# Between two decoder layers: squares on GpSimd, weight splits behind three sigmoids, and fillers of 512 and 256 columns

## The chip, the cores and the metric

The kernel runs on 1 core of a Trainium2 chip. The metric is the device time of one execution in microseconds (us). The engines of the core that matter here are TensorE (PE in the profile, with PEld for its weight loads), VectorE (DVE), ScalarE (ACT), GpSimd (POOL) and the queue of SyncE (SP) that issues the loads.

## The reference

One inference step of a decoder with two layers, 320 tokens (a prompt of 256 and 8 samples of 8), 1024 features. Each layer is four sub-layers with a norm before and after each; the last one is the one that the change touches:

```python
def rmsnorm(x, g):
    return x * lax.rsqrt(jnp.mean(x * x, axis=-1, keepdims=True) + EPS) * g
...
for i in range(DEPTH):                      # DEPTH = 2
    f = swiglu(rmsnorm(h, P['g_f1_pre'][i]), ...)
    h = h + 0.5 * rmsnorm(f, P['g_f1_post'][i])
    mo = mixer(rmsnorm(h, P['g_mix_pre'][i]), ...)
    h = h + rmsnorm(mo, P['g_mix_post'][i])
    f = swiglu(rmsnorm(h, P['g_f2_pre'][i]), ...)
    h = h + 0.5 * rmsnorm(f, P['g_f2_post'][i])
    gate = jax.nn.sigmoid(rmsnorm(h, P['g_ple_pre'][i]) @ P['w_ple_gate'][i])
    h = h + rmsnorm((p[i] @ P['w_ple_proj'][i]) * gate, P['g_ple_post'][i])
return rmsnorm(h, P['g_final'])
```

## The kernel before

Activations lie with features on the 128 partitions and the 320 tokens along the free dimension, so a row of 1024 features is 8 tiles of 128x320. Every product is made of three fp32r matmuls (high part by high part, high by low, low by high), so each weight and each activation is split into a high part (a copy on ScalarE, `w_hi_sb`, `x_hi`) and a low part (a subtraction on VectorE, `w_lo_sb`, `x_lo`). All order is written out by hand: each engine has its own program, and counting semaphores join them.

Weights stream through four slots (j = 0 to 3) of 128x1024. For each half, SyncE loads `raw`, ScalarE's `split` copies it to `w_hi_sb`, VectorE's `split` makes `w_lo_sb`, and TensorE uses it. A slot's next high part waits until TensorE is done with that slot (`halves_done`), and SyncE reloads `raw` when the low parts of its two slots are there (`w_lo`).

The phase `pg` is the product with `w_ple_gate`: two pairs of four halves, one output tile m = 0 to 7 for each half. For each tile VectorE takes the product out of PSUM (`move` into `ga`, semaphore `moved`), ScalarE applies the sigmoid (`sg`), and VectorE multiplies the tile of `gate` by it (`embed`, semaphore `ple_out`). The norm behind it (`post4`) needs the sum of squares of all 8 tiles of `gate`. Before the change ScalarE squares tiles 0 to 6 (`square`, into one of two buffers `sq`), VectorE adds them into `ssq` (`add_square`, semaphore `summed`), and VectorE squares tile 7 itself (semaphore `squared`). TensorE sums both over partitions (`sums`: three matmuls on `ssq` after `summed`, three on `sq` after `squared`), ScalarE takes the root (`finish_root`), VectorE inverts it (`invert`), TensorE spreads it over the partitions (`spread`), and VectorE's `boundary` scales and adds the 8 tiles to `h` and starts the next layer's first product (`first_pair` of the phase `f1_up`). Its first three weight halves (slots 0 to 2) have to be split before it, the fourth comes later.

`keep_warm` issues matmuls whose result nobody reads (fillers), with as many columns as it is told. They stand in TensorE's program between the steps of `sums` and `spread`, behind the waits that come before them. After the first sub-layer (`post1`, once in each layer) there are fillers before and after `spread` too.

Layer 1 is the last one: it ends in another way (`L == LAST`), and there is one such passage from `pg` to the next layer's `f1_up` in the whole program.

Of the kernel before, what the change touches and what calls it, by code (L numbers as in the profile page):

```python
# [110 lines left out]
def trunk(nc, x, par, side, early, w_proj, g_rows, streams, y, states):  # L111
    with ExitStack() as ctx:
# [119 lines left out]
        pool_sq = sem("pool_sq")  # L232
        x_lo_pool = sem("x_lo_pool")
# [226 lines left out]
        def _(pe):  # L460
            WARM_SIG, WARM_ROOT, WARM_X = 6, 3, 9
# [103 lines left out]
            def sums(L, name):  # L565

                n = WT if name == "ln" else DT
                tailed = name in TAILED
                pe.wait_ge(summed, v_sq(L, name, n - 1))
                for t in range(3):  # L570
                    mm = pe.matmul(ps[:, STATB, t:t + 1], ssq[:, t * P:(t + 1) * P], ones[:, 0:1], start=t == 0,  # L571
                                   stop=not tailed, skip_group_check=True)
                if tailed:

                    if name == "post4":
                        keep_warm(WARM_ROOT)
                    pe.wait_ge(squared, v_sq(L, name, n - 1))
                    for t in range(3):
                        n = min(P, T - t * P)
                        mm = pe.matmul(ps[0:n, STATB, t:t + 1], sq[:, 1, t * P:t * P + n], ones[:, 0:1], start=False,  # L580
                                       stop=True, skip_group_check=True)
                mm.then_inc(stat_full, 1)
# [132 lines left out]
            for L in range(DEPTH):  # L715
# [10 lines left out]
                keep_warm(WARM_ROOT)  # L726
                spread(L, "post1")
                keep_warm(WARM_X, T // 2)
# [85 lines left out]
                if L < LAST:  # L814
                    keep_warm(WARM_SIG)
                    sums(L, "post4")
                    keep_warm(WARM_ROOT)
                    spread(L, "post4")
                    keep_warm(WARM_X, T // 2)
# [5 lines left out]
        def _(act):  # L825
# [203 lines left out]
            for L in range(DEPTH):  # L1029
# [94 lines left out]
                for m in range(DT):  # L1124
                    if m == 2:
                        split(L, "pg", 1, 3)
                    sigmoid(sg[:, m % RING3, :], ga[:, m % 2, :], L, "pg", m)
                    for q in ((m - 1,) if m < 4 else (m - 1, m) if m == 4 else (m,) if m < DT - 1 else ()):
                        if q >= 0:
                            act.wait_ge(ple_out, L * DT + q + 1)  # L1130
                            square(gate[:, q, :], L, "post4", q, q % 2)
                            if L == LAST:
                                gain(L, q)
                    if 4 <= m < DT - 1:
                        if nxt_layer:
                            split(*nxt_layer, m - 4)
                        else:
                            keep_turned(m - 2)
# [28 lines left out]
        def _(dve):  # L1167
# [39 lines left out]
            def boundary(L, n, b, post, pre, gain, nxt):  # L1207
# [31 lines left out]
                if n == 3:  # L1239
                    split(*nxt, 1)  # L1240
# [5 lines left out]
                if n == 3:  # L1246
                    split(*nxt, 2)
# [174 lines left out]
            for L in range(DEPTH):  # L1422
# [139 lines left out]
                for m in range(DT):  # L1562
# [8 lines left out]
                    if 2 <= m <= 4:  # L1571
                        add_square(L, "post4", m - 2, m % 2)
                    if m >= 4:
                        add_square(L, "post4", m - 1, (m - 1) % 2)
# [4 lines left out]
                    if m in (1, 3):  # L1579
                        split(L, "pg", 1, 2 if m == 1 else 3)  # L1580
                    if m == 5 and nxt_layer:
                        split(*nxt_layer, 0)
                dve.wait_ge(ple_out, L * DT + DT)
                dve.wait_ge(summed, v_sq(L, "post4", DT - 3))
                if L == LAST:
                    dve.tensor_tensor(LAST_SQ[:, 0:T], gate[:, DT - 1, :], gate[:, DT - 1, :], ALU.mult)
                    dve.tensor_tensor(LAST_SQ[:, T:TPAD], gate[:, DT - 1, 2 * P:T], gate[:, DT - 1, 2 * P:T], ALU.mult).then_inc(squared, 1)
                else:
                    dve.tensor_tensor(sq[:, 1, :], gate[:, DT - 1, :], gate[:, DT - 1, :], ALU.mult).then_inc(squared, 1)
# [20 lines left out]
        def _(pool):  # L1610
# [21 lines left out]
            def boundary_x(L, n):  # L1632
                for m in POOL_X:
# [4 lines left out]
                    if n == 2 and m:  # L1638
# [4 lines left out]
                        pool.tensor_tensor(CHASE_SQ[0], CHASE_SQ[0], CHASE_SQ[i], ALU.add).then_inc(pool_sq, 1)  # L1643

# [62 lines left out]
            for L in range(DEPTH):  # L1707
# [84 lines left out]
                if L + 1 < DEPTH:  # L1792
                    boundary_x(L, 3)
# [125 lines left out]
```

## Time and profile before

| what | value |
|---|---|
| three timed executions | 1550.05, 1550.15 and 1550.22 us (median 1550.15) |
| span of the profiled execution, first to last instruction | 1547.5 us |
| median of the timed executions above that span | 2.65 us |
| TensorE busy | 1530.3 us, 99% of the span |
| VectorE, ScalarE, GpSimd busy | 1038.2, 717.9 and 652.3 us (67%, 46%, 42%) |
| mean granted TensorE clock | 0.995 of full |

The profiled execution has no total listed apart from its span; what lies around the span (start and end of the program) is taken from the timed executions. A line such as L1172 is a line of the kernel; the line of a helper stands for all its uses. In a timeline a row has the start, the duration, the engine, the line, the operation with output and inputs, and in brackets how long the engine had been idle and who released it.

### The profile page before, as it was taken

The numbers are of one execution on the slowest core, as the hardware profiler recorded it, in microseconds if no ns is written. First come the engines' busy times: TensorE is split into PE (matmuls) and PEld (weight loads), VectorE is DVE, ScalarE is ACT, GpSimd is POOL, SyncE is SP. The second block draws the span as 40 slices with busy tenths as digits, with TensorE's granted clock in tenths as the row PEclk, the third lists the DMA queues.
The fourth block names the chain that finished last, engine by engine and source line by source line (L and its number), as shares of the span: only waits on it lengthen the run. The fifth ranks groups of instructions, "written<-read, shape, count | busy, mean of one in ns | idle before, by whom it ended". The sixth has DMA issues, their size and how long they took to land.

```text
span 1547.5 us, 27988 instructions
## 1 busy us (share of the span) xinstructions
PE 1530.3 (99%) x10370; PEld 1521.0 (98%) x10370; DVE 1038.2 (67%) x1577; ACT 717.9 (46%) x1064; POOL 652.3 (42%) x693
## 2 busy tenths in 40 slices
PE   9999999999999999999999999999999999999997
PEld 9999999999999999999999999999999999999997
DVE  7555437999886755634885554389998876555356
ACT  6333335445466433433663333355455654334346
POOL 3755203499321555500147551045973317554011
PEclk9999999999999999999999999999999999999998
DMA  6444432444443544532334454334444335445422
GB/s 221 163 160 173 180 129 82 164 144 157 163 148 110 186 162 137 209 141 102 125 129 161 145 193 169 119 109 141 160 163 137 132 125 191 157 140 204 143 73 82
DMA packets 53208, 229.29 MB, mean 148 GB/s; under 512 B 3856, under 2 KB 3984, under 8 KB 49040
## 3 DMA queue, kind: packets, MB, share of 16 engines
q1 hardware_dynamic: 52560, 226.07, 42.6%
q10 hardware_dynamic: 576, 2.26, 0.4%
q8 instruction: 45, 0.74, 0.2%
q14 instruction: 27, 0.22, 0.0%
HBM read 225.27 MB, written 3.04 MB: 148 GB/s over the span
## 4 chain that ended last, share of the span: by engine, by line
PE 95%; DVE 3%; issue 1%; ACT 1%; POOL 0%; DVEq 0%; POOLq 0%; ACTq 0%
PE ps L467 29%; PE ps L469 29%; PE ps L468 29%; PE ps L509 1%; PE ps L505 1%; PE ps L506 1%; DVE h L1222 1%; DVE ga L1217 0%; DVE w_lo_sb L1172 0%; PE ps L541 0%; POOL x_lo L1637 0%; PE ps L646 0%; PE ps L587 0%; PE ps L571 0%; PE ps L647 0%
## 5 line engine op out<-in xcount | busy, mean ns | idle before, releaser
L1172 DVE TENSOR_TENSOR w_lo_sb<-raw,w_hi_sb 128x1024 fp32r<-128x1024 f32 (+1 forms) x388 | 552.9, 1426 | 227.5 <-ACT w_hi_sb L832 227.0
L467 PE MATMUL ps<-x_hi,w_hi_sb 128*128 128x320 f32 x2232 | 693.3, 311 | 1.7 <-DVE w_lo_sb L1172 1.7
L832 ACT ACTIVATE w_hi_sb<-raw 128x1024 fp32r<-128x1024 f32 (+1 forms) x388 | 429.1, 1111 | 564.6 <-PE ps L469 477.5
L469 PE MATMUL ps<-x_hi,w_lo_sb 128*128 128x320 f32 x2232 | 689.6, 309 | 0.0
L468 PE MATMUL ps<-x_lo,w_hi_sb 128*128 128x320 f32 x2232 | 689.6, 309 | 0.0
L467 PEld LDWEIGHTS ps<-x_hi,w_hi_sb 128*128 128x128 f32 x2232 | 419.0, 188 | 4.0 <-DVE w_lo_sb L1172 2.5
L468 PEld LDWEIGHTS ps<-x_lo,w_hi_sb 128*128 128x128 f32 x2232 | 419.0, 188 | 0.8
L469 PEld LDWEIGHTS ps<-x_hi,w_lo_sb 128*128 128x128 f32 x2232 | 419.0, 188 | 0.0
L467 PE MATMUL ps<-mid_hi,w_hi_sb 128*128 128x320 f32 x704 | 217.4, 309 | 0.0
L468 PE MATMUL ps<-mid_lo,w_hi_sb 128*128 128x320 f32 x704 | 217.4, 309 | 0.0
L469 PE MATMUL ps<-mid_hi,w_lo_sb 128*128 128x320 f32 x704 | 217.4, 309 | 0.0
L1637 POOL TENSOR_TENSOR x_lo<-pmf,x_hi 128x320 fp32r<-128x320 f32 x14 | 14.4, 1027 | 404.0 <-ACT pmf L879 251.5
L1622 POOL TENSOR_TENSOR gb<-ga,gb 128x320 f32<-128x320 f32 x88 | 79.9, 908 | 213.9 <-DVE gb L1299 213.8
L1625 POOL TENSOR_TENSOR gb<-gb,sg 128x320 f32<-128x320 f32 x88 | 146.2, 1661 | 15.6 <-POOL gb L1622 12.6
L1299 DVE TENSOR_TENSOR ga<-ps,rb 128x320 f32<-128x320 f32 x168 | 81.5, 486 | 95.9 <-PE ps L469 68.1
L467 PEld LDWEIGHTS ps<-mid_hi,w_hi_sb 128*128 128x128 f32 x704 | 132.2, 188 | 0.0
L469 PEld LDWEIGHTS ps<-mid_hi,w_lo_sb 128*128 128x128 f32 x704 | 132.2, 188 | 0.0
L468 PEld LDWEIGHTS ps<-mid_lo,w_hi_sb 128*128 128x128 f32 x704 | 132.2, 188 | 0.0
L1372 DVE SCALAR_TENSOR_TENSOR ps<-cbuf,cur,ps 128x256 f32<-128x256 f32 x348 | 108.1, 378 | 0.0
L1299 DVE TENSOR_TENSOR gb<-ps,rb 128x320 f32<-128x320 f32 x104 | 50.7, 487 | 55.5 <-PE ps L469 55.4
L1630 POOL TENSOR_TENSOR mid_lo<-gb,mid_hi 128x320 f32 x88 | 81.6, 927 | 14.7 <-POOL mid_hi L1628 14.7
L837 ACT ACTIVATE sq<-ps 128x320 f32<-128x320 f32 x48 | 21.0, 437 | 113.8 <-PE ps L469 113.8
(223 smaller groups left out, 1642.8 us busy)
## 6 DMA issues: line engine op xcount, KB each, us to landing
raw<-in_w_f_up SPq DMA_DIRECT2D x86, 1024.0 KB, 5.2
raw<-in_w_f_dn SPq DMA_DIRECT2D x32, 1408.0 KB, 6.0
raw<-in_w_gate SPq DMA_DIRECT2D x24, 1024.0 KB, 5.2
raw<-in_w_out SPq DMA_DIRECT2D x12, 1024.0 KB, 5.3
raw<-in_w_glu SPq DMA_DIRECT2D x8, 1024.0 KB, 5.2
raw<-in_w_short SPq DMA_DIRECT2D x8, 1024.0 KB, 5.3
raw<-in_w_wo SPq DMA_DIRECT2D x8, 1024.0 KB, 5.3
raw<-in_w_pg SPq DMA_DIRECT2D x8, 1024.0 KB, 5.3
```

Of the source, the lines that this page charges most:

```text
L467: pe.matmul(out, whi, rhs_hi, start=start, stop=False, skip_group_check=True)
L468: pe.matmul(out, whi, rhs_lo, start=False, stop=False, skip_group_check=True)
L469: return pe.matmul(out, wlo, rhs_hi, start=False, stop=stop, skip_group_check=True)
L505: pe.matmul(out, w_hi_sb[:, j, w], x_hi[:, k, :], start=k == 0, stop=False, skip_group_check=True)
L832: act.activation(w_hi_sb[:, j, 0:n], raw[:, j, 0:n], ACT.Copy).then_inc(w_hi, 1)
L837: act.activation(sq[:, par, :], src, ACT.Square).then_inc(squared, 1)
L1172: dve.tensor_tensor(w_lo_sb[:, j, 0:n], raw[:, j, 0:n], w_hi_sb[:, j, 0:n].bitcast(F32), ALU.subtract).then_inc(w_lo, 1)
L1299: dve.tensor_tensor(out, ps[:, bank, 0:T], rb[:, :], ALU.mult).then_inc(moved, 1)
L1372: dve.scalar_tensor_tensor(dst, src, cur[:, c:c + 1], before, ALU.mult, ALU.add).then_inc(tap, 1)
L1622: pool.tensor_tensor(gb[:, g, :], ga[:, g, :], gb[:, g, :], ALU.mult).then_inc(swi, 1)
L1625: pool.tensor_tensor(gb[:, g, :], gb[:, g, :], sg[:, g, :], ALU.mult).then_inc(swi, 1)
L1630: pool.tensor_tensor(lo, gb[:, g:g + 1, :], hi.bitcast(F32), ALU.subtract).then_inc(mid_ready, 1)
```

## The change

In the passage from layer 0 to layer 1, GpSimd squares tiles 0 to 6 of `gate` and adds them up (new function `gate_squares`), two instructions for each tile but the first; ScalarE no longer squares there and VectorE no longer adds. ScalarE's high parts for the next layer's slots 0, 1 and 2 stand right behind the sigmoids of tiles 3, 5 and 6, and VectorE's low parts behind the `embed` of tiles 5 (slot 0) and 6 (slots 1 and 2), where the latter two stood in `boundary` before. The fourth half of `pg` is split one tile earlier on both engines. The fillers get new numbers and widths, and those ahead of the first three matmuls of `sums` go. Layer 1 keeps its own way of doing all this, but for the fillers of `post1`.

```diff
-            WARM_SIG, WARM_ROOT, WARM_X = 6, 3, 9
+            WARM_SIG, WARM_SQRT, WARM_X, WARM_COLS = 6, 2, 5, 512
+            WARM_ROOT, WARM_ROOT_COLS = 4, 256
...
                     if name == "post4":
-                        keep_warm(WARM_ROOT)
+                        keep_warm(WARM_SIG, WARM_COLS)
                     pe.wait_ge(squared, v_sq(L, name, n - 1))
...
                 sums(L, "post1")
-                keep_warm(WARM_ROOT)
+                keep_warm(WARM_ROOT, WARM_ROOT_COLS)
                 spread(L, "post1")
-                keep_warm(WARM_X, T // 2)
+                keep_warm(WARM_X, WARM_COLS)
...
                 if L < LAST:
-                    keep_warm(WARM_SIG)
                     sums(L, "post4")
-                    keep_warm(WARM_ROOT)
+                    keep_warm(WARM_SQRT, WARM_COLS)
                     spread(L, "post4")
-                    keep_warm(WARM_X, T // 2)
+                    keep_warm(WARM_X, WARM_COLS)
...
                 for m in range(DT):
-                    if m == 2:
+                    if m == (1 if nxt_layer else 2):
                         split(L, "pg", 1, 3)
                     sigmoid(sg[:, m % RING3, :], ga[:, m % 2, :], L, "pg", m)
+                    if nxt_layer:
+                        if m in (3, 5, 6):
+                            split(*nxt_layer, {3: 0, 5: 1, 6: 2}[m])
+                        continue
...
-                if n == 3:
-                    split(*nxt, 1)
                 invert(L, post)
...
-                if n == 3:
-                    split(*nxt, 2)
                 dve.wait_ge(bc_full, v_bc(L, post))
...
-                    if m in (1, 3):
-                        split(L, "pg", 1, 2 if m == 1 else 3)
-                    if m == 5 and nxt_layer:
-                        split(*nxt_layer, 0)
+                    if m == 1:
+                        split(L, "pg", 1, 2)
+                    if m == (2 if nxt_layer else 3):
+                        split(L, "pg", 1, 3)
+                    if nxt_layer and m in (5, 6):
+                        for j in ((0,), (1, 2))[m - 5]:
+                            split(*nxt_layer, j)
...
+            def gate_squares(L):
+
+                wait_alone(stat_full, v_stat(L, "pre3"))
+                for q in range(DT - 1):
+                    if q:
+                        wait_alone(summed, v_sq(L, "post4", q - 1))
+                    pool.wait_ge(ple_out, L * DT + q + 1)
+                    pool.tensor_tensor(sq[:, 0, :] if q else ssq[:, 0:T], gate[:, q, :], gate[:, q, :], ALU.mult
+                                       ).then_inc(pool_square if q else summed, 1)
+                    if q:
+                        pool.wait_ge(pool_square, L * (DT - 2) + q)
+                        pool.tensor_tensor(ssq[:, 0:T], ssq[:, 0:T], sq[:, 0, :], ALU.add).then_inc(summed, 2 if q == DT - 2 else 1)
```

VectorE, layer 0, from the `move` of tile 5 to the first step of `boundary`; as it was before (rows on `ssq` are `add_square`; the first row on `w_lo_sb` is slot 0, the one behind `sq<-gate` slot 1, and slot 2 follows behind a reciprocal):

```order
L1299 TENSOR_TENSOR ga<-ps,rb 128x320
L1186 TENSOR_TENSOR ssq<-ssq,sq 128x320
L1559 TENSOR_TENSOR gate<-gate,sg 128x320
L1172 TENSOR_TENSOR w_lo_sb<-raw,w_hi_sb 128x1024
L1299 TENSOR_TENSOR ga<-ps,rb 128x320
L1186 TENSOR_TENSOR ssq<-ssq,sq 128x320
L1559 TENSOR_TENSOR gate<-gate,sg 128x320
L1299 TENSOR_TENSOR ga<-ps,rb 128x320
L1186 TENSOR_TENSOR ssq<-ssq,sq 128x320
L1559 TENSOR_TENSOR gate<-gate,sg 128x320
L1589 TENSOR_TENSOR sq<-gate 128x320
L1172 TENSOR_TENSOR w_lo_sb<-raw,w_hi_sb 128x1024
```

The same place with the change; the row x2 holds slots 1 and 2:

```order
L1296 TENSOR_TENSOR ga<-ps,rb 128x320
L1556 TENSOR_TENSOR gate<-gate,sg 128x320
L1173 TENSOR_TENSOR w_lo_sb<-raw,w_hi_sb 128x1024
L1296 TENSOR_TENSOR ga<-ps,rb 128x320
L1556 TENSOR_TENSOR gate<-gate,sg 128x320
L1173 TENSOR_TENSOR w_lo_sb<-raw,w_hi_sb 128x1024 x2
L1296 TENSOR_TENSOR ga<-ps,rb 128x320
L1556 TENSOR_TENSOR gate<-gate,sg 128x320
L1590 TENSOR_TENSOR sq<-gate 128x320
L1191 RECIPROCAL rinv<-root 128x3
```

The additions are gone, and the splits of slots 1 and 2 moved from behind the square of tile 7 to ahead of tile 7's `move`.

TensorE at the end of `pg` in layer 0, before (the last product of `pg`, then fillers on `pw_hi`, `sums` on `ssq` and `sq`, `spread` on `rinv`, and the first product of `f1_up`):

```order
L469 MATMUL ps<-x_hi,w_lo_sb 128x320
L563 MATMUL ps<-p_hi,pw_hi 128x320 x6
L571 MATMUL ps<-ones,ssq 128x1 x3
L563 MATMUL ps<-p_hi,pw_hi 128x320 x3
L580 MATMUL ps<-ones,sq 128x1 x2
L580 MATMUL ps<-ones,sq 64x1
L563 MATMUL ps<-p_hi,pw_hi 128x320 x3
L594 MATMUL ps<-ident,rinv 128x128 x3
L563 MATMUL ps<-p_hi,pw_hi 128x160 x9
L505 MATMUL ps<-x_hi,w_hi_sb 128x320
```

The same place with the change:

```order
L471 MATMUL ps<-x_hi,w_lo_sb 128x320
L573 MATMUL ps<-ones,ssq 128x1 x3
L565 MATMUL ps<-p_hi,pw_hi 128x512 x6
L582 MATMUL ps<-ones,sq 128x1 x2
L582 MATMUL ps<-ones,sq 64x1
L565 MATMUL ps<-p_hi,pw_hi 128x512 x2
L596 MATMUL ps<-ident,rinv 128x128 x3
L565 MATMUL ps<-p_hi,pw_hi 128x512 x5
L507 MATMUL ps<-x_hi,w_hi_sb 128x320
```

No filler stands between `pg` and the matmuls on `ssq` any more, and the six between those on `ssq` and those on `sq` are 512 columns wide.

## Rows read from the trace of the kernel before

**Rows 1.** The page: chain that ended last, share of the span by engine.

```profile
PE 95%; DVE 3%; issue 1%; ACT 1%; POOL 0%; DVEq 0%; POOLq 0%; ACTq 0%
```

**Rows 2.** Timeline of PE from the end of `pg` to `f1_up`.

```profile
764.44 1.04 PE L563 MATMUL ps<-p_hi,pw_hi 128*128 128x320 f32 x6
766.06 0.83 PE L571 MATMUL ps<-ones,ssq 128*128 128x1 f32 x6 [0.58 <-DVE ssq L1186]
...
767.83 0.91 PE L580 MATMUL ps<-ones,sq 128*128 128x1 f32 x6 [0.40 <-DVE sq L1589]
...
769.63 0.84 PE L594 MATMUL ps<-ident,rinv 128*128 128x128 f32 x3
770.12 2.19 PE L563 MATMUL ps<-p_hi,pw_hi 128*128 128x160 f32 x9
772.15 0.61 PE L505 MATMUL ps<-x_hi,w_hi_sb 128*128 128x320 f32 x1
```

**Rows 3.** Timeline of DVE in the same passage.

```profile
752.77 0.49 DVE L1559 TENSOR_TENSOR gate<-gate,sg 128x320 f32<-128x320 f32 x1 [0.42 <-ACT sg L932]
753.18 1.22 DVE L1172 TENSOR_TENSOR w_lo_sb<-raw,w_hi_sb 128x1024 fp32r<-128x1024 f32 x1
...
764.83 0.48 DVE L1299 TENSOR_TENSOR ga<-ps,rb 128x320 f32<-128x320 f32 x1
765.51 0.49 DVE L1186 TENSOR_TENSOR ssq<-ssq,sq 128x320 f32<-128x320 f32 x1 [0.20 <-issue]
766.76 0.49 DVE L1559 TENSOR_TENSOR gate<-gate,sg 128x320 f32<-128x320 f32 x1 [0.76 <-ACT sg L932]
767.28 0.49 DVE L1589 TENSOR_TENSOR sq<-gate 128x320 f32<-128x320 f32 x1
...
770.51 0.49 DVE L1217 TENSOR_TENSOR ga<-gate,ps 128x320 f32<-128x320 f32 x1 [0.15 <-PE ps L594]
```

**Rows 4.** Timeline of ACT around the sigmoid of tile 7.

```profile
765.33 1.04 ACT L832 ACTIVATE w_hi_sb<-raw 128x1024 fp32r<-128x1024 f32 x1
766.27 0.45 ACT L932 ACTIVATE sg<-ga 128x320 f32<-128x320 f32 x1
```

**Rows 5.** Windows: stretch, its us, busy of PE, PEld, DVE, ACT, POOL, then PEclk.

```profile
768.00:769.00 1.00, 1.00 (x7) 0.97 (x8) 0.91 (x1) 0.25 (x3) 0.00 (x0) 0.65 0.09 16
775.00:776.00 1.00, 1.00 (x8) 1.00 (x8) 0.96 (x3) 1.00 (x3) 0.12 (x1) 0.93 0.00 0
```

**Rows 6.** Two lines of POOL (duration min/median/max in ns), and POOL's timeline there.

```profile
L1622 POOL TENSOR_TENSOR gb<-ga,gb x88: 876/887/1865, 27.9 to 1416.3; 128x320 f32<-128x320 f32 x88
...
L1628 POOL CAST mid_hi<-gb x88: 451/452/1395, 30.9 to 1419.8; 128x320 f32 x88
...
772.45 0.87 POOL L1637 TENSOR_TENSOR x_lo<-pmf,x_hi 128x320 fp32r<-128x320 f32 x1 [28.25 <-ACT pmf L879]
```

**Rows 7.** Timeline of POOL, three instructions elsewhere in layer 0 and 1.

```profile
439.58 1.06 POOL L1783 TENSOR_TENSOR cc<-cc,sg 128x320 f32<-128x320 f32 x1 [0.26 <-DVE cc L1529]
...
736.46 0.88 POOL L1637 TENSOR_TENSOR x_lo<-pmf,x_hi 128x320 fp32r<-128x320 f32 x1 [1.63 <-ACT pmf L879]
...
853.35 1.67 POOL L1625 TENSOR_TENSOR gb<-gb,sg 128x320 f32<-128x320 f32 x1 [0.16 <-POOL gb L1622]
```

**Rows 8.** Timeline of DVE at the same three moments.

```profile
439.42 1.56 DVE L1532 TENSOR_TENSOR cc<-cc,sg 128x320 f32<-128x320 f32 x2
...
736.49 0.48 DVE L1217 TENSOR_TENSOR ga<-f,ps 128x320 f32<-128x320 f32 x1
...
852.83 1.45 DVE L1172 TENSOR_TENSOR w_lo_sb<-raw,w_hi_sb 128x1024 fp32r<-128x1024 f32 x1 [0.60 <-ACT w_hi_sb L832]
```

**Rows 9.** Timeline of PE behind the first sub-layer of layer 0.

```profile
243.44 0.54 PE L594 MATMUL ps<-ident,rinv 128*128 128x128 f32 x3
243.74 1.21 PE L563 MATMUL ps<-p_hi,pw_hi 128*128 128x160 f32 x9
245.60 0.39 PE L505 MATMUL ps<-x_hi,w_hi_sb 128*128 128x320 f32 x1 [0.65 <-DVE x_hi L1257]
```

More of the change, by code:

```diff
@@ L232, in trunk @@
         pool_sq = sem("pool_sq")
+        pool_square = sem("pool_square")
         x_lo_pool = sem("x_lo_pool")
@@ L1131, in _ @@
                             square(gate[:, q, :], L, "post4", q, q % 2)
-                            if L == LAST:
-                                gain(L, q)
+                            gain(L, q)
                     if 4 <= m < DT - 1:
[L1135 to L1138, printed above, removed]
+                        keep_turned(m - 2)
                 act.preload_act_table(ACT.Sqrt)
@@ L1570, in _ @@
                         embed(m - 1)
-                    if 2 <= m <= 4:
+                    if 2 <= m <= 4 and L == LAST:
                         add_square(L, "post4", m - 2, m % 2)
                     if m >= 4:
-                        add_square(L, "post4", m - 1, (m - 1) % 2)
+                        if L == LAST:
+                            add_square(L, "post4", m - 1, (m - 1) % 2)
                         if L == LAST and m == DT - 1:
@@ L1578, in _ @@
                         embed(m)
-                    if m in (1, 3):
-                        split(L, "pg", 1, 2 if m == 1 else 3)
-                    if m == 5 and nxt_layer:
-                        split(*nxt_layer, 0)
+                    if m == 1:
[5 more added lines that the diff above has]
+                            split(*nxt_layer, j)
                 dve.wait_ge(ple_out, L * DT + DT)
-                dve.wait_ge(summed, v_sq(L, "post4", DT - 3))
                 if L == LAST:
+                    dve.wait_ge(summed, v_sq(L, "post4", DT - 3))
                     dve.tensor_tensor(LAST_SQ[:, 0:T], gate[:, DT - 1, :], gate[:, DT - 1, :], ALU.mult)
@@ L1588, in _ @@
                 else:
-                    dve.tensor_tensor(sq[:, 1, :], gate[:, DT - 1, :], gate[:, DT - 1, :], ALU.mult).then_inc(squared, 1)
+                    dve.tensor_tensor(sq[:, 1, :], gate[:, DT - 1, :], gate[:, DT - 1, :], ALU.mult).then_inc(squared, DT)
                 if nxt_layer:
@@ L1792, in _ @@
                 if L + 1 < DEPTH:
+                    gate_squares(L)
                     boundary_x(L, 3)
```

## The prediction, made before the changed kernel ran

> **What bounds the kernel now.** I read the chain that ended last first: TensorE holds 95% of it [rows 1]. An edit on the other engines can only pay where TensorE waits for them. The change touches one such place, the passage from `pg` of layer 0 to `f1_up` of layer 1, and the fillers of `post1`; so I read TensorE's timeline there next. The fillers behind the last product start at 764.44, the first product of layer 1 at 772.15 [rows 2]: 7.7 us in which TensorE does nothing that counts. All that the change can win or lose lies there.
>
> What ends those waits: the matmuls on `ssq` start at 766.06, when VectorE's last addition ends (765.51 + 0.49 = 766.00), those on `sq` at 767.83, when tile 7's square ends (767.28 + 0.49 = 767.77) [rows 2, 3]. Behind them root, reciprocal and `spread` run to VectorE's first step at 770.51, and from there it is 772.15 - 770.51 = 1.64 us to the product [rows 2, 3]. So the chain is: tile 7's `move` (764.83), its sigmoid (766.27), its `embed` (766.76), its square. The sigmoid could have followed the `move` at 765.31, but ScalarE's weight split stood ahead of it from 765.33 on [rows 3, 4]; that costs about 0.9 us. The clock: 0.65 of full over 768 to 769 means that it fell to half (1.2 GHz) at about 768.3, and 0.93 over 775 to 776 that it rose to 2.4 GHz at about 775.1 [rows 5]; TensorE had gaps before the fall and ran almost without any before the rise. GpSimd is idle for 28 us until 772.45 [rows 6].
>
> **The change, part by part.** Removed: seven squares on ScalarE, seven additions on VectorE. Taken alone that frees the chain: the sigmoid of tile 7 no longer stands behind a split.
>
> GpSimd's new work is 13 instructions on 128x320. One such instruction takes 0.88 us where nothing disturbs it [rows 6], and the next, which waits for its result, starts 0.16 us later [rows 7]; where the semaphore goes through `wait_alone` I take 0.20. So a tile costs 0.88 + 0.16 + 0.88 + 0.20 = 2.1 us, against 0.49 on VectorE. Tile 0's `embed` ends at 753.26 [rows 3], tile 1's about 755.2, and six tiles from there end at 755.4 + 6 x 2.1 = about 767.8 even if nothing disturbs them: 1.8 us after the 766.00 of now. GpSimd sets the time of `ssq`, not the sigmoids.
>
> It will be disturbed. A GpSimd instruction at 853.35 took 1.67 us, 0.79 over its 0.88, while VectorE's split ran from 852.83 to 854.28: it got going 0.14 us before the split's end [rows 7, 8]. At 439.58 one took 1.06, and the second of two VectorE products, asked for at about 439.83, ended at 439.42 + 1.56 = 440.98, where two alone take 0.9: here VectorE waited for GpSimd [rows 7, 8]. At 736.46 one took its plain 0.88 beside a VectorE instruction that read PSUM (736.49) [rows 7, 8]. So instructions of the two engines that read two SBUF tiles take turns, in order of asking. In this passage VectorE has such ones in plenty: eight `embed`, tile 7's square (0.49 each) and five splits (1.22 each) [rows 3].
>
> I walked through the passage with these durations: turns in order of asking, handed over 0.14 us before the end, other waits as in the rows. The splits of `pg` hold up tiles 0 and 1 (tile 0's square ends 755.1, tile 1's addition 758.4). Additions 2 to 6 then end at about 760.6, 763.8, 767.0, 769.9 and 772.0. VectorE is held up in its turn: slot 0's split ends at 763.1, `embed` 6 at 764.5, the splits of slots 1 and 2 at 766.3 and 768.1, and only then come tile 7's `move` (768.5 against 765.31 now), its sigmoid (769.0), `embed` (770.2) and square (771.3). With 0.16 in place of 0.20 the two ends are 771.3 and 772.2; with handovers from 0.05 to 0.3 us before the end, 770.5 to 774 and 769.4 to 773. I take **772.0 for `ssq`**, square of tile 7 at or ahead of it.
>
> The Trainium skill's page "SBUF — State Buffer", section "Who interferes with whom", says that the second engine blocks fully until the first finishes. The rows at 853.35 show 0.14 us less than that [rows 7, 8]. By the page's rule the same walk ends at 774.0 and the time below would be 2 us longer.
>
> Next TensorE. Its program now has no filler between `pg` (764.44) and the wait for `ssq`, so it stands idle for 7.5 us, longer than any gap now, and the clock is at half when the matmuls on `ssq` start. Six fillers of 512 columns follow. They were to cover the wait for tile 7's square, but that square is there already: they stand on the path. No row has 512 columns: six of 320 took 1.04 us, of which about 0.15 each and 0.3 for the last to drain [rows 2], so 512 columns are 0.24 us at full clock by the ratio of columns and 0.47 at half; I bound one by 0.15 (as 320) and 0.47. From 772.0 at half clock: six passes on `ssq` 1.4 (0.83 at full clock, scaled by `spread`, 0.84 against 0.54 [rows 2, 9], and up to double), fillers 2.8, passes on `sq` 1.4, root and reciprocal as now (768.74 to 769.25, 0.5) while two more fillers run 0.9, `spread` 0.84, then 1.64 to the product: 781.0, which is 8.8 later than 772.15. All at full clock: 0.83 + 1.4 + 0.83 + 0.5 + 0.54 + 1.64 = 5.7, so 777.8, 5.6 later. In the passage as it is now the clock came back to full while such matmuls ran without gaps [rows 5], so I expect it back somewhere within these 9 us and take 7.0, the middle. The next layer's first tiles then run at full clock, but GpSimd's `x_lo` tiles at 772.45 and after still pace them [rows 6]: 0.2 back.
>
> Nothing else counts. Behind GpSimd's squares the next layer's `x_lo` tiles are queued; the first of them waits for the first `h` tile, which comes 5 us after the squares are done. In `post1` TensorE's nine fillers end at 244.95 and it waits for `x_hi` until 245.60 [rows 9]; five of 512 take 1.3 us from 243.74 and end at 245.04, still before. Four of 256 columns have 1024 in all, where three of 320 have 960: 0.03 us. If that cover were gone, each `post1` would cost 0.1. Loads: slot 2 was split at 765.33 without a wait for its load [rows 4]; its load now starts about 1.1 us earlier, with the earlier split of `pg`'s fourth half, and the split comes no more than that earlier. ScalarE's extra splits lie between sigmoids where it is idle; the one between sigmoids 0 and 1 delays `embed` 1 by nothing, since VectorE is in a split until 754.40 [rows 3].
>
> Sum: + 7.0 - 0.2 = + 6.8 us. The span of the profiled execution, 1547.5, becomes 1554.3; the timed median lies 2.65 above the span, so 1550.15 + 6.8 = **1557.0 us**. From TensorE's start in layer 1 all is bound by TensorE as before, so that the shift stays to the end.
>
> **The rivals.**
>
> *GpSimd and VectorE don't hinder each other here.* Then `ssq` is there at 767.8 and tile 7's square at 767.2. Speaks for it: many GpSimd instructions keep the 0.88, the median of L1622 is 887 ns [rows 6]. Against: the stretched ones fall just where VectorE reads two SBUF tiles [rows 7, 8]. The time: 767.8 + 5.7 = 773.5 at full clock (+ 1.3), or, since the clock now falls at 768.3 anyway, the fillers at half, up to + 3.6. So 1551.5 to 1553.8, 1552.3 as the likeliest.
>
> *GpSimd keeps pace, and it is not slower.* A product of a tile with itself might cost what a cast of one tile does, 0.45 [rows 6], and take no turns. Then a tile costs 0.45 + 0.16 + 0.88 + 0.2 = 1.7, `ssq` is there at 765.5, the fillers run at full clock till 767.8 and hide the square. Then passes 0.83, chain 0.5, `spread` 0.54, 1.64: 771.3, 0.85 earlier, 1549.3. It decides from 1.7 us for a tile downward. Against it: the square reads two operands, as L1622 does.
>
> *The clock doesn't fall,* as the fillers are there for: then my 7.0 is 5.6 and the time 1555.5, inside my range.
>
> **How the numbers follow.** Forecast (turns, GpSimd the bound) 0.80, between 1554 (770.5 and full clock all along, + 3.9) and 1559.5; no hindrance 0.12; GpSimd keeps pace 0.05; later than 1559.5 (handover at the very end, clock late) 0.03. A measurement of this kernel can tell about 0.2%, 3.1 us, from no change. Slower by more: the forecast, the last case and a little of the second, 0.83; within: 0.15; faster by over 3.1 us, which no case reaches, 0.02. The range from 1552.5 to 1559.8 leaves out the third case, half of the second and some of the last.
>
> **What would show it.** In the trace after: GpSimd's additions 2.4 to 3.5 us apart and the last ending near 772, several of its instructions over 1.2 us; tile 7's `move` after 767.5, behind two splits stretched beyond 1.22; TensorE idle from 764.4 to about 772, six wide fillers at once behind the matmuls on `ssq`, with the wait for tile 7's square short or none; clock at half from about 768 on; first product of layer 1 at 777 to 781; `post1` unchanged. It is wrong if the additions keep to 2.1 us or less, if tile 7's square comes before 768, or if the wide fillers hide behind a wait.

## The result and the profile after

The changed kernel takes 1555.47 us (median of five executions, 1555.26 to 1555.89) against 1550.08 us (five, 1549.20 to 1550.22): ratio 1.0037, 95% interval 1.0027 to 1.0048, so 5.4 us slower. The forecast was 1557.0 us, 1.5 us more. The span of the profiled execution went from 1547.5 to 1553.5 us.

I call **passage** the time from the start of the last product of `pg` to the start of the first product of `f1_up`. It was 7.86 us (764.29 to 772.15) and is 14.78 us, 6.92 more. The timeline of TensorE after the change, from the last product of `pg` (L471) on, answers to [rows 2]:

```profile
763.73 0.31 PE L471 MATMUL ps<-x_hi,w_lo_sb 128*128 128x320 f32 x1
769.64 1.44 PE L573 MATMUL ps<-ones,ssq 128*128 128x1 f32 x6 [5.60 <-POOL ssq L1657]
770.94 2.91 PE L565 MATMUL ps<-p_hi,pw_hi 128*128 128x512 f32 x6
773.64 1.15 PE L582 MATMUL ps<-ones,sq 128*128 128x1 f32 x6
774.72 1.22 PE L565 MATMUL ps<-p_hi,pw_hi 128*128 128x512 f32 x2
775.74 0.84 PE L596 MATMUL ps<-ident,rinv 128*128 128x128 f32 x3
776.23 2.48 PE L565 MATMUL ps<-p_hi,pw_hi 128*128 128x512 f32 x5
778.51 0.47 PE L507 MATMUL ps<-x_hi,w_hi_sb 128*128 128x320 f32 x1
```

Two things are to be seen. In front there is one gap of 5.60 us, which ends when GpSimd has `ssq` ready; before, fillers stood there and VectorE's `ssq` ended a gap of 0.58 [rows 2]. Behind it, nothing waits: no bracket stands at the six wide fillers or at the passes on `sq`, so these six take 773.64 - 770.94 = 2.70 us of the path.

What GpSimd does meanwhile, from its timeline (L1653 squares a tile, L1657 adds it), from the addition of tile 2 to that of tile 6:

```profile
758.58 1.01 POOL L1657 TENSOR_TENSOR ssq<-ssq,sq 128x320 f32<-128x320 f32 x1
759.77 0.72 POOL L1653 TENSOR_TENSOR sq<-gate 128x320 f32<-128x320 f32 x1 [0.18 <-POOL ssq L1657]
760.57 1.01 POOL L1657 TENSOR_TENSOR ssq<-ssq,sq 128x320 f32<-128x320 f32 x1
761.75 1.48 POOL L1653 TENSOR_TENSOR sq<-gate 128x320 f32<-128x320 f32 x1 [0.18 <-POOL ssq L1657]
763.32 0.88 POOL L1657 TENSOR_TENSOR ssq<-ssq,sq 128x320 f32<-128x320 f32 x1
764.38 0.75 POOL L1653 TENSOR_TENSOR sq<-gate 128x320 f32<-128x320 f32 x1 [0.18 <-POOL ssq L1657]
765.20 1.72 POOL L1657 TENSOR_TENSOR ssq<-ssq,sq 128x320 f32<-128x320 f32 x1
767.10 1.48 POOL L1653 TENSOR_TENSOR sq<-gate 128x320 f32<-128x320 f32 x1 [0.18 <-POOL ssq L1657]
768.73 0.86 POOL L1657 TENSOR_TENSOR ssq<-ssq,sq 128x320 f32<-128x320 f32 x1
```

And VectorE in the same stretch, which answers to [rows 3]:

```profile
760.76 1.90 DVE L1173 TENSOR_TENSOR w_lo_sb<-raw,w_hi_sb 128x1024 fp32r<-128x1024 f32 x1
762.58 0.48 DVE L1296 TENSOR_TENSOR ga<-ps,rb 128x320 f32<-128x320 f32 x1
763.60 0.95 DVE L1556 TENSOR_TENSOR gate<-gate,sg 128x320 f32<-128x320 f32 x1 [0.54 <-ACT sg L933]
764.47 3.53 DVE L1173 TENSOR_TENSOR w_lo_sb<-raw,w_hi_sb 128x1024 fp32r<-128x1024 f32 x2
767.92 0.48 DVE L1296 TENSOR_TENSOR ga<-ps,rb 128x320 f32<-128x320 f32 x1
768.94 0.99 DVE L1556 TENSOR_TENSOR gate<-gate,sg 128x320 f32<-128x320 f32 x1 [0.54 <-ACT sg L933]
770.04 0.49 DVE L1590 TENSOR_TENSOR sq<-gate 128x320 f32<-128x320 f32 x1
```

GpSimd never idles for more than 0.18 us between these instructions and its last addition ends at 769.59; it is the last to arrive at `ssq`. Its row of 1.72 (765.20) and the two squares of 1.48 (761.75 and 767.10) fall beside VectorE's splits (760.76 and 764.47), which are longer in turn: 1.90, and 3.53 for two, where one took 1.22 [rows 3]. The `move` of tile 7 (767.92) reads PSUM and keeps its 0.48, but stands behind those splits.

The granted clock, by windows (columns as in [rows 5]):

```profile
767.00:768.00 1.00, 0.00 (x0) 0.00 (x0) 1.00 (x2) 0.00 (x0) 0.91 (x1) 1.00 0.19 33
768.00:769.00 1.00, 0.00 (x0) 0.00 (x0) 0.46 (x2) 0.55 (x2) 0.85 (x2) 0.83 0.84 184
769.00:778.00 9.00, 8.36 (x27) 7.12 (x28) 2.91 (x6) 2.69 (x4) 0.58 (x1) 0.50 0.23 92
779.00:780.00 1.00, 1.00 (x8) 0.91 (x7) 1.00 (x2) 0.18 (x1) 0.43 (x1) 1.00 0.07 16
```

It fell from 2.4 to 1.2 GHz within 768 to 769 (0.83 there), while TensorE was idle, and stood at 0.50 from 769 to 778; from 779 on it is full. So everything between `ssq` and the first product runs at half.

The timed difference is smaller than 6.92 because of three other parts. From the first product of layer 1 to the one behind its `post1` 0.34 came back (238.16 us against 238.50). All that lies ahead of the passage ran 0.56 earlier in this execution (763.73 against 764.29); 0.52 of it is there already at `post1`'s wide fillers (243.22 against 243.74), ahead of which only four fillers of `post1` differ, so it is no gain of this passage. Nor is it more than the scatter: in the traces shown below the last product of `pg` starts between 763.40 and 765.05. And 1555.47 - 1553.5 = 1.97 lies around the span, 0.68 less than the 2.65 of before. That is no gain either: in every later execution with both figures on record, of whichever kernel, 1.75 to 2.24 lies around the span, and the 2.65 compares the median of the timed executions with the span of another one. 6.92 - 0.34 - 0.56 - 0.68 = 5.3, for the 5.4 measured.

`post1` was costed at nothing. Its wide fillers and the product behind them, after the change:

```profile
243.22 1.40 PE L565 MATMUL ps<-p_hi,pw_hi 128*128 128x512 f32 x5
245.09 0.39 PE L507 MATMUL ps<-x_hi,w_hi_sb 128*128 128x320 f32 x1 [0.47 <-DVE x_hi L1254]
```

They run 0.19 us longer than the nine of before, and the wait behind them is 0.47 in place of 0.65 [rows 9]: from the first filler to the product 1.87 us now, 1.86 before. The wait for `x_hi` swallows it.

### The profile page after: what moved, and what is told of

It is laid out like the page before. It is cut to its first block, busy times and chain, and to the rows that moved or that the text cites. A ratio compares the mean times of both kernels' runs of the same rounds, so it can differ in the third digit from the quotient of the medians.

```text
span 1553.5 us, 27954 instructions
## 1 busy us (share of the span) xinstructions
PE 1531.6 (99%) x10356; PEld 1519.8 (98%) x10356; DVE 1038.4 (67%) x1570; ACT 714.3 (46%) x1057; POOL 666.8 (43%) x706
## 4 chain that ended last, share of the span: by engine, by line
PE 93%; DVE 3%; POOL 1%; issue 1%; ACT 1%; DMA 1%; SPq 0%; DVEq 0%; POOLq 0%; ACTq 0%
PE ps L469 29%; PE ps L471 29%; PE ps L470 29%; PE ps L511 1%; PE ps L508 1%; PE ps L507 1%; DVE h L1223 1%; DVE ga L1218 0%; POOL sq L1653 0%; POOL ssq L1657 0%; DMA h<-in_x 0%; PE ps L573 0%; POOL x_lo L1638 0%; DMA raw<-in_w_f_up 0%; PE ps L565 0%
## 5 line engine op out<-in xcount | busy, mean ns | idle before, releaser
L471 PE MATMUL ps<-x_hi,w_lo_sb 128*128 128x320 f32 x2232 | 689.6, 309 | 0.0
L471 PEld LDWEIGHTS ps<-x_hi,w_lo_sb 128*128 128x128 f32 x2232 | 419.0, 188 | 0.0
L471 PE MATMUL ps<-mid_hi,w_lo_sb 128*128 128x320 f32 x704 | 217.4, 309 | 0.0
L471 PEld LDWEIGHTS ps<-mid_hi,w_lo_sb 128*128 128x128 f32 x704 | 132.2, 188 | 0.0
```

Of the source, the lines that this page charges most:

```text
L471: return pe.matmul(out, wlo, rhs_hi, start=False, stop=stop, skip_group_check=True)
```

## The experiments

Every passage is read as above. A word on the method: a part of the change that costs 1 us here is 0.06% of the time, so the passage in the trace says more than the ratio, and the ratio is the cross-check. "Excess" is the passage less 7.86; "timed" is the median less the median of the kernel before on the same chip (1549.42, 1549.31 and 1549.57 us in the three groups, 21 to 31 executions each; 2 executions for "GpSimd late", 7 to 11 for the others).

| kernel | passage us | excess us | timed us | ratio (95%) |
|---|---|---|---|---|
| the change | 14.78 | 6.92 | +5.4 | 1.0037 (1.0027 to 1.0048) |
| change without the six fillers | 12.21 | 4.35 | +4.4 | 1.0028 (1.0018 to 1.0037) |
| change with 24 fillers in the wait | 11.62 | 3.76 | +3.6 | 1.0020 (1.0011 to 1.0030) |
| both of these | 10.49 | 2.63 | +2.7 | 1.0017 (1.0008 to 1.0027) |
| GpSimd alone | 9.72 | 1.86 | +2.7 | 1.0013 (1.0004 to 1.0023) |
| splits alone | 8.52 | 0.66 | +1.2 | 1.0011 (1.0002 to 1.0021) |
| fillers alone | 9.26 | 1.40 | +1.1 | 1.0006 (0.9996 to 1.0016) |
| splits and fillers, no GpSimd | 10.30 | 2.44 | +3.4 | 1.0018 (1.0008 to 1.0027) |
| GpSimd and splits, old fillers | 12.73 | 4.87 | +4.7 | 1.0031 (1.0020 to 1.0041) |
| GpSimd and fillers, old splits | 12.23 | 4.37 | +4.5 | 1.0027 (1.0016 to 1.0039) |
| GpSimd late (waits for all tiles) | 23.58 | 15.72 | +15.1 | 1.0094 (1.0076 to 1.0113) |
| before, sigmoids first | 6.74 | -1.12 | -0.8 | 0.9994 (0.9985 to 1.0004) |

A passage is that of one execution, and the clock does not fall at the same place in each. In the change it fell 4.9 us behind the start of the last product, without the six fillers 2.4 us, although what TensorE was given is the same up to there and it was idle at both moments. So where the clock falls near the passes on `ssq` or behind them, two passages can differ by that moment alone. For "GpSimd alone" the traced execution is the shortest of its ten (1550.91, median 1552.15), for "GpSimd and fillers" the shortest of seven (1552.85, median 1553.78): these two passages are likely to lie on the low side. The intervals of the ratio reach about 1.5 us to either side, and those of the change, of "without the six fillers" and of "24 fillers in the wait" overlap: what sets these apart is read from the traces.

**The theory** at this point: GpSimd is late with `ssq` because it and VectorE take turns; the late `ssq` leaves TensorE idle, the clock falls, and the chain behind runs at half clock with six fillers on the path. **Rivals**: the fillers or the splits cost it and GpSimd's lateness is by the way; or GpSimd is just slow and no turns are taken.

**Without the six fillers** (against the changed kernel):

```diff
-                        keep_warm(WARM_SIG, WARM_COLS)
+                        keep_warm(0, WARM_COLS)
```

> The changed kernel without the six fillers of 512 columns between the matmuls on ssq and those on sq. 'Passage' is the time from the start of pg's last product to the start of f1_up's first: 7.86 us before, 14.78 with the change. Theory (late ssq makes the loss, and the six fillers stand bare on the path at half clock): the matmuls on ssq start at 5.9 into the passage as with the change, those on sq follow at once, at about 7.2 in place of 9.92, and the passage shrinks by about 2.7 to 12.1; 1552.8 us. Rival (the fillers hide behind the wait for tile 7's square): passage 14 to 14.8.

The passage is 12.21, 2.57 shorter; `ssq` comes 5.90 us behind the last product, as in the change (5.91). The passes on `sq` follow those on `ssq` at once and wait for nothing (timeline of TensorE):

```profile
770.21 1.44 PE L573 MATMUL ps<-ones,ssq 128*128 128x1 f32 x6 [5.59 <-POOL ssq L1657]
771.50 1.29 PE L582 MATMUL ps<-ones,sq 128*128 128x1 f32 x6
```

So the six fillers hide nothing: tile 7's square is there before `ssq` is used.

**24 fillers in the wait** (against the changed kernel), to keep the clock up while GpSimd works:

```diff
                 if L < LAST:
+                    keep_warm(24, WARM_COLS)
                     sums(L, "post4")
```

> The changed kernel with 24 fillers of 512 columns more, ahead of the matmuls on ssq, where TensorE is idle for 5.6 us. Theory (the half clock costs about 3.3 us of the loss, and the idle stretch is what the clock falls after): the fillers take 5.3 us and end before ssq is there, so the matmuls on ssq still start at 5.9; clock full through the passage; from ssq to the first product 5.6 in place of 8.9; passage 11.5; 1552.2 us. Rival (the chain of waits alone counts, the clock does not): passage over 14.3 at either clock.

The passage is 11.62, 3.16 shorter. `ssq` is as late as in the change (5.95); the clock keeps 1.00 in both windows, and the same passes, fillers and steps take less:

```profile
764.00:768.00 4.00, 4.00 (x23) 3.51 (x22) 3.46 (x4) 1.42 (x2) 3.67 (x4) 1.00 0.02 6
772.00:777.00 5.00, 4.48 (x24) 3.34 (x23) 2.05 (x6) 1.77 (x3) 0.03 (x1) 1.00 0.07 29
```

TensorE's rows of the same kernel:

```profile
765.19 5.63 PE L565 MATMUL ps<-p_hi,pw_hi 128*128 128x512 f32 x24
771.00 0.83 PE L573 MATMUL ps<-ones,ssq 128*128 128x1 f32 x6 [0.18 <-POOL ssq L1658]
771.69 1.65 PE L565 MATMUL ps<-p_hi,pw_hi 128*128 128x512 f32 x6
...
776.66 0.38 PE L507 MATMUL ps<-x_hi,w_hi_sb 128*128 128x320 f32 x1 [0.52 <-DVE x_hi L1255]
```

From `ssq` to the product it is 5.66 us here and 8.87 in the change: half the clock costs 3.2. The passes on `ssq` take 0.83 and not 1.44. Nine of this kernel's ten executions have a mean clock of 0.997, the five of the change 0.993 to 0.995.

**Both of these**, the two edits together.

> The changed kernel with both repairs of TensorE's program: 24 wide fillers ahead of the matmuls on ssq, none of the six between those and the ones on sq. Theory (what is left then is GpSimd's late ssq alone): ssq at 5.9 into the passage, clock full, passes 0.7 and 0.7, the rest 3.0 to 2.8: passage about 10.1, still 2.2 over the kernel before; 1551.5 us. If the fillers and the clock made all of the loss: passage 8 or less.

10.49: with the clock kept and the six fillers gone, 2.63 over before remain. `ssq` comes at 5.95, against 1.77 before, and nothing else in this passage is worse than before: that remainder is GpSimd's lateness, less what the old passage lost between `ssq` and tile 7's square and to its own half clock.

**GpSimd alone**: the kernel before with `gate_squares` and without the squares on ScalarE and the additions on VectorE in this passage; splits and fillers as before.

```diff
-                        if q >= 0:
+                        if q >= 0 and L == LAST:
...
-                        add_square(L, "post4", m - 1, (m - 1) % 2)
+                        if L == LAST:
+                            add_square(L, "post4", m - 1, (m - 1) % 2)
...
+                    gate_squares(L)
```

> The kernel before with GpSimd's squares and additions alone: splits and fillers stay where they were. Theory (GpSimd's own rate and its turns with VectorE make ssq late, wherever the splits stand): with only three of the five splits beside it, ssq is there at about 4.9 into the passage (1.77 before, 5.91 with the change), tile 7's square at about 5.3, the passage is about 11.5, 3.6 longer than before; 1553.7 us. Rival (the splits put ahead of tile 7 make the loss): ssq at about 2, passage 8 to 9, within 1 us of the kernel before.

9.72, less than expected: `ssq` comes at 4.29 (4.9 was expected), and in this execution the clock is still at full when the passes on `ssq` start; it falls at about 769.6, 6.0 us behind the last product. TensorE's rows, and the window of the fall:

```profile
763.83 1.04 PE L564 MATMUL ps<-p_hi,pw_hi 128*128 128x320 f32 x6
767.98 0.83 PE L572 MATMUL ps<-ones,ssq 128*128 128x1 f32 x6 [3.10 <-POOL ssq L1658]
769.00:770.00 1.00, 1.00 (x10) 0.97 (x8) 0.41 (x1) 0.00 (x0) 0.00 (x0) 0.82 0.06 16
```

GpSimd is slower than the old way without any other part of the change (the ratio, 1.0004 to 1.0023, says so too), but `ssq` is 1.6 us earlier than with the new splits.

**No GpSimd**: the changed kernel with the squares back on ScalarE and the additions back on VectorE.

```diff
-                    gate_squares(L)
...
-                        if L == LAST:
-                            add_square(L, "post4", m - 1, (m - 1) % 2)
+                        add_square(L, "post4", m - 1, (m - 1) % 2)
```

> The changed kernel with the squares back on ScalarE and the additions back on VectorE; splits and fillers as in the change. Theory (GpSimd makes most of the loss): ssq at about 3.3 into the passage, passage 9 (full clock) to 11 (half clock), so 4 to 6 of the 6.9 us lost come back; 1550 to 1552 us. Rival (splits and fillers make the loss): ssq later than 4.5, passage 13 or more.

10.30: the other two parts are a loss without GpSimd too, 2.44 us. The next two kernels part them.

**Splits alone**: the same, with the fillers of before.

```diff
-            WARM_SIG, WARM_SQRT, WARM_X, WARM_COLS = 6, 2, 5, 512
-            WARM_ROOT, WARM_ROOT_COLS = 4, 256
+            WARM_SIG, WARM_ROOT, WARM_X = 6, 3, 9
...
-                        keep_warm(WARM_SIG, WARM_COLS)
+                        keep_warm(WARM_ROOT)
...
+                    keep_warm(WARM_SIG)
                     sums(L, "post4")
-                    keep_warm(WARM_SQRT, WARM_COLS)
+                    keep_warm(WARM_ROOT)
                     spread(L, "post4")
-                    keep_warm(WARM_X, WARM_COLS)
+                    keep_warm(WARM_X, T // 2)
```

> The kernel before with the new places of the weight splits alone (squares on ScalarE, additions on VectorE, old fillers). Passage 7.86 before, 14.78 with the whole change. If the parts add up and the splits ahead of tile 7's move are a part of the loss: ssq at 3.3 into the passage (as in the run without GpSimd), tile 7's square at 4.4, then 4.0 to 4.3 as before, passage 8.4 to 8.8. If the splits are harmless: 7.9 or less.

8.52. The rows to read are VectorE's two splits and TensorE's wait, which VectorE ends 1.5 us later than in [rows 2]:

```profile
764.61 2.35 DVE L1173 TENSOR_TENSOR w_lo_sb<-raw,w_hi_sb 128x1024 fp32r<-128x1024 f32 x2
767.82 0.83 PE L572 MATMUL ps<-ones,ssq 128*128 128x1 f32 x6 [2.08 <-DVE ssq L1187]
```

VectorE's last addition stands behind tile 7's `move`, and that stands behind the splits of slots 1 and 2, 2.35 us long here. It is the pair of splits that the change moved on VectorE, without any turns.

**Fillers alone**: the kernel before with the new counts, places and widths, that is the diff just shown the other way round.

> The kernel before with the new fillers alone. ssq at 1.8, passes to 2.5, six wide fillers to 3.9, just past tile 7's square (3.5), so the matmuls on sq start at about 3.9 to 4.0; then the rest with two and five wide fillers, at half clock up to 0.5 longer: passage 8.4 to 9.0. If the fillers are what loses by themselves: 10 or more.

9.26, a little over what was expected (8.4 to 9.0). `ssq` comes as early as before (1.76), but six wide fillers take 2.0 us between it and `sq` and outlast the wait that they stand in; the passes on `sq` start 0.85 us later (4.39 against 3.54), and at half clock:

```profile
766.41 2.15 PE L564 MATMUL ps<-p_hi,pw_hi 128*128 128x512 f32 x6
768.36 1.15 PE L581 MATMUL ps<-ones,sq 128*128 128x1 f32 x6
```

The half clock is that of this execution, in which it fell at about 767.3. The times do not tell this kernel from the one before (0.9996 to 1.0016): four of its ten executions took 1548.6 to 1549.1 us at a mean clock of 0.996 to 0.997, the traced one and five more 1550.3 to 1552.8 at 0.994 to 0.995. That the fillers lose by themselves is shown for the traced execution alone.

**GpSimd and splits**: the changed kernel with the fillers of before, by the same diff.

> The changed kernel with the old fillers, so GpSimd's squares and the splits' new places together. ssq at 5.9 as with the change; passes 1.3, three fillers 0.8, passes and the rest 4.4: passage about 12.4 if the parts of the loss act through ssq and what stands behind it. If the two added up as they do alone (1.86 for GpSimd, under 1 for the splits): 10.5.

**GpSimd and fillers**: the kernel of "GpSimd alone" with the fillers of the change.

> The kernel before with GpSimd's squares and the new fillers, splits at their old places. ssq at 4.3 (as with GpSimd alone), clock at half by then since no filler stands ahead of it, passes 1.3, six fillers 2.6, the rest 4.9: passage about 12.5 to 13.1; at full clock 10.5. If what counts is the splits' new place: under 10.

The two passages are 12.73 and 12.23. Alone the two parts of each pair sum to 1.86 + 0.66 = 2.52 and 1.86 + 1.40 = 3.26; together they cost 4.87 and 4.37. TensorE's wait with GpSimd and splits, and the window in which the clock falls:

```profile
769.98 1.44 PE L572 MATMUL ps<-ones,ssq 128*128 128x1 f32 x6 [4.73 <-POOL ssq L1657]
767.00:768.00 1.00, 0.00 (x0) 0.00 (x0) 1.00 (x1) 0.00 (x0) 0.82 (x2) 0.62 0.00 0
```

`ssq` comes at 5.92 and not 4.29, and the clock has fallen before it: these passes take 1.44 where they take 0.83 with GpSimd alone. But it fell 3.2 us behind the last product here and 6.0 there, with the same six fillers ahead of the wait and TensorE idle behind them until 4.29 in both. So the fall at 3.2 is not the splits' doing, and the old fillers do not keep the clock up. With GpSimd and fillers, where no filler stands ahead of the wait, the clock was expected at half by then, and it was not:

```profile
767.80 0.83 PE L573 MATMUL ps<-ones,ssq 128*128 128x1 f32 x6 [3.98 <-POOL ssq L1658]
```

By the passages all three parts alone sum to 3.92, and together they cost 6.92. By the medians they sum to 2.7 + 1.2 + 1.1 = 5.0, and together they cost 5.4. That the parts cost more where they meet than they do alone is therefore not shown.

**GpSimd late**: the changed kernel, in which GpSimd begins only when all eight gate tiles are there. This takes its work out of VectorE's way, at a price that is known beforehand.

```diff
                 wait_alone(stat_full, v_stat(L, "pre3"))
+                wait_alone(ple_out, L * DT + DT)
```

> The changed kernel in which GpSimd's squares wait until all eight tiles of gate are there, so that they run beside nothing on VectorE; it is a measurement of the disputed cost, not a candidate. Theory (instructions that read two SBUF tiles take turns): every embed of VectorE is 0.49 and every split 1.22 again, tile 7's move starts at about 1 into the passage (4.2 with the change) and its square ends at about 3; GpSimd's squares are 0.75 and its additions 0.88 without one longer than 1.1, so 13 of them take about 12.2 and ssq is there at about 15; passage about 24. Rival (GpSimd's long instructions and VectorE's long splits are slow by themselves): the 1.5 to 1.7 us instructions and the 1.7 to 1.9 us splits stay.

Now VectorE's splits of slots 1 and 2 and tile 7's `move` and square read:

```profile
762.09 2.36 DVE L1173 TENSOR_TENSOR w_lo_sb<-raw,w_hi_sb 128x1024 fp32r<-128x1024 f32 x2
764.37 0.48 DVE L1296 TENSOR_TENSOR ga<-ps,rb 128x320 f32<-128x320 f32 x1
...
765.98 0.49 DVE L1590 TENSOR_TENSOR sq<-gate 128x320 f32<-128x320 f32 x1
```

and GpSimd's first square, the next pair, and its last addition:

```profile
766.05 0.99 POOL L1654 TENSOR_TENSOR ssq<-gate 128x320 f32<-128x320 f32 x1 [22.75 <-DVE gate L1556]
767.23 0.72 POOL L1654 TENSOR_TENSOR sq<-gate 128x320 f32<-128x320 f32 x1 [0.18 <-POOL ssq L1654]
768.02 0.86 POOL L1658 TENSOR_TENSOR ssq<-ssq,sq 128x320 f32<-128x320 f32 x1
...
777.25 0.86 POOL L1658 TENSOR_TENSOR ssq<-ssq,sq 128x320 f32<-128x320 f32 x1
```

The two splits take 2.36 in place of 3.53, tile 7's `move` starts 0.97 us behind the last product's start in place of 4.20, and GpSimd's instructions are 0.72 and 0.86, but for the first (0.99), which shares its time with tile 7's square. GpSimd's additions are (777.25 - 768.02) / 5 = 1.85 us apart, against 2.0 to 2.7 in the change (from end to end). Each engine is as fast alone as it was taken to be, or faster, and both are slower together: the turns are shown, from both sides.

**Before, sigmoids first**: a version of the kernel before that uses one idea of the change, that the splits on ScalarE go behind the sigmoids (here of tiles 3, 5 and 7, ahead of the squares), with the split of `pg`'s fourth half one tile earlier on ScalarE as in the change, and leaves VectorE's order and the fillers alone.

```diff
-                    if m == 2:
+                    if m == (1 if nxt_layer else 2):
                         split(L, "pg", 1, 3)
                     sigmoid(sg[:, m % RING3, :], ga[:, m % 2, :], L, "pg", m)
+                    if nxt_layer and m in (3, 5, 7):
+                        split(*nxt_layer, {3: 0, 5: 1, 7: 2}[m])
...
-                    if 4 <= m < DT - 1:
-                        if nxt_layer:
-                            split(*nxt_layer, m - 4)
-                        else:
-                            keep_turned(m - 2)
+                    if 4 <= m < DT - 1 and L == LAST:
+                        keep_turned(m - 2)
```

> The kernel before with one thing of the change in another form: ScalarE's high parts right behind the sigmoids of tiles 3, 5 and 7 (not 6), ahead of the squares; squares stay on ScalarE, additions and low parts where VectorE had them, old fillers. Theory (the split ahead of tile 7's sigmoid costs 0.9 us in the kernel before): tile 7's sigmoid follows its move at once, its square ends at about 2.2 to 2.5 into the passage in place of 3.5, passage 6.4 to 7.0, so 0.9 to 1.4 us faster; about 1548.5 us. Rival (the delayed squares or the split of slot 2 behind the sigmoid become the bound): passage 7.8 or more.

ScalarE's rows, where before the split stood ahead of the sigmoid [rows 4]:

```profile
764.84 0.47 ACT L932 ACTIVATE sg<-ga 128x320 f32<-128x320 f32 x1 [0.64 <-DVE ga L1298]
765.22 1.04 ACT L832 ACTIVATE w_hi_sb<-raw 128x1024 fp32r<-128x1024 f32 x1
```

The sigmoid of tile 7 follows its `move` (764.31 + 0.49) at once, and the passage is 6.74 us, 1.12 shorter than before. The time, 0.9994 (0.9985 to 1.0004), is not told from no change by this measurement; that it is faster as a whole is not shown.

## Why the prediction was right, and two steps that were not

The sign, the place and the mechanism hold: GpSimd sets `ssq`, turns with VectorE make it late, TensorE idles, the clock falls and the wide fillers stand on the path. The size, + 6.8 forecast and + 5.4 measured, is better than its terms. For the first product the forecast was 7.0 us later, and it came 6.92 later, from two errors that cancel, which is luck:

- **`ssq` at 772.0** was 1.9 us too late. The last addition ended at 769.59, which is 769.59 + 0.56 = 770.15 on the time axis of before, just under the lower end of the bounds (770.5). The term that was mis-sized is the GpSimd tile, "0.88 + 0.16 + 0.88 + 0.20 = 2.1": a square of a tile with itself takes 0.72 where nothing disturbs it, its addition starts about 0.1 us behind it (767.23 + 0.72 to 768.02 in "GpSimd late"), and an undisturbed tile is 1.85. The 0.88 was taken from an instruction with two different tiles [rows 6]. From tile 2 on this makes 4 x 0.25 = 1.0 of the 1.9; 0.4 to 0.5 was there by tile 2 already, and the rest is in the turns. GpSimd's additions 2 to 6 ended 2.0, 2.6, 2.7 and 2.7 us apart, where the walk had 3.2, 3.2, 2.9 and 2.1 (and its sign was 2.4 to 3.5): over an undisturbed tile that is 2.6 us of turns in place of 3.0, on tiles 4 to 6 and not on tiles 3 to 5. VectorE's side came as walked: tile 7's `move` at 767.92 + 0.56 = 768.5 (forecast 768.5), its square ending at 770.53 + 0.56 = 771.1 (forecast 771.3).
- **The chain from `ssq` to the first product** was taken as 7.0 us later, the middle between 5.6 (full clock) and 8.8 (half). The clock did not come back within the chain: from the passes on `ssq` to the product it took 8.87, for which the forecast had 9.0 at half clock. Choosing the middle (which is 7.2, not 7.0) was the error, 1.7 us; the estimate of each case was good, since with the clock kept it took 5.66, for 5.7 forecast.

The fillers at half clock, "2.8" for six, took 2.70. The 0.2 given back in layer 1 were 0.34. `post1` cost nothing. Nearly all of the 1.5 us by which the forecast was too high lies outside the passage: the 0.56 ahead of it, which no step had and which is scatter, and the 0.68 around the span, where the step "the timed median lies 2.65 above the span" took the difference of two executions for a property of the program.

The rivals: *no hindrance* fell by "GpSimd late", in which both engines' instructions shrink once they no longer meet. *GpSimd keeps pace* fell by its own condition: even undisturbed a tile takes 1.85, and it was to decide from 1.7 downward. *The clock doesn't fall* fell by the windows, and "24 fillers in the wait" shows what it would have been worth, 3.2 us.

The rule of the Trainium skill (page "SBUF — State Buffer", section "Who interferes with whom"), that one engine blocks the other fully, agrees with these rows in kind, but not to the end of the instruction. GpSimd's square at 761.75 ended at 763.23, and its own 0.72 before that is 762.51, 0.15 ahead of the split's end (760.76 + 1.90 = 762.66). The square at 767.10 gives 0.14 in the same way (768.58 - 0.72 = 767.86, and the splits end at 768.00): the handover of 0.14 read from [rows 7, 8] holds here.

What the parts cost, from the experiments, is what the prediction had not asked. The new splits are a loss by themselves (0.66 in the passage, and a ratio of 1.0002 to 1.0021), and they make GpSimd's `ssq` 1.6 us later. The six wide fillers behind the passes on `ssq` cost 2.57 in the change; that the new fillers lose without GpSimd is not told by the times. The prediction had counted on a gain, "Taken alone that frees the chain": "before, sigmoids first" shows that ScalarE's part, in another form, is one in the passage (1.12), and "splits alone" that all of the change's splits together, those of VectorE ahead of tile 7's `move` among them, lose 0.66. The splits were not moved one by one.

## What to carry to other kernels

Work that is moved to an idle engine is worth what that engine takes for it while its neighbour runs, not alone: look first at which of the neighbour's instructions read two SBUF tiles in the same stretch, and count each such pair as taking turns. Fillers belong in front of the wait that ends last, and enough of them to fill it: 24 wide ones kept the clock here, the six old ones of "GpSimd and splits" did not. Behind that wait they are work on the path, and at half clock twice as dear. Where a forecast has a clock that changes "somewhere in between", price the two cases and state both, rather than take the middle. And where the clock falls at another place in each execution, don't take the difference of two single traces for the worth of a part before the times agree with it.

## What the runs showed of the hardware

- GpSimd multiplies a tile of 128x320 with itself in 0.72 to 0.75 us and adds two tiles in 0.86 to 0.88, undisturbed.
- GpSimd and VectorE take turns on instructions that read two SBUF operands: VectorE's two splits took 3.53 us beside GpSimd and 2.36 without it, GpSimd's square took 1.48 and its addition 1.72 beside splits, 0.72 and 0.86 undisturbed. VectorE's `move`, which reads PSUM, kept its 0.48.
- The clock fell at a different distance from the last product in each execution: 4.9 us in the change, 2.4 without the six fillers and 3.0 with GpSimd late, where TensorE had the same work up to the fall; 3.2 and 6.0 with the six old fillers ahead of the wait ("GpSimd and splits", "GpSimd alone").
- The clock did not come back during the chain: it was 0.50 over 769 to 778, with TensorE busy for 8.36 of these 9 us, so that the first product of `f1_up` still began at half clock (0.47 us, against 0.31 for one at full clock).
- A filler of 512 columns is 5.63 / 24 = 0.23 us apart at full clock, and 2.70 / 6 = 0.45 at half; six passes on a single column take 0.83 and 1.44.
